# A hybrid decoder layer pair on one core: recurrent gates, norm sums and spreads placed between the last eight projection units, compression weights in eight pieces

## The chip, the core and the metric

One core of one Trainium2 chip runs the whole program in one launch. The metric is device time in microseconds (us) of that core. The engines are TensorE (PE; its weight loads are shown apart as PEld), VectorE (DVE), ScalarE (ACT), GpSimd (POOL) and SyncE (SP), which here only issues DMAs. The engines run their own instruction streams in order and meet at semaphores.

## What is computed

Two layers, each a mixer followed by a convolutional feed-forward part, over 320 tokens at once (256 of a prompt, and 8 sequences of 8 new tokens). Only the first mixer, a gated delta rule with 16 value heads and 8 key heads, and the compression weights of the second mixer are touched. In outline (q, k, v are slices of one projection; the recurrence is done in chunks):

```
h = rms_norm(x, gdn_norm)
qkv, z, b, a = split(h @ gdn_w_in)            # 4096 + 2048 + 16 + 16 columns
qkv = silu(causal_dwconv(qkv, conv_buf, conv_w))
q, k = l2norm(q) * DK ** -0.5, l2norm(k)      # over the 128 channels of a head
beta = sigmoid(b);  g = -exp(a_log) * softplus(a + dt_bias)
o = gated delta rule(q, k, v, g, beta, state) # per head; new states are outputs
y = (rms_norm(o) * out_norm * silu(z)) @ gdn_w_out
...
block = silu(blocks_of(past k or v, + cmp_pe) @ cmp_w1) @ cmp_w2     # second mixer
```

`cmp_pe` enters as a bias: `cmp_pe @ cmp_w1`, four columns of 128, is computed once.

## The kernel before, in words

The projection `gdn_in` is 24 units of 256 output columns (line 735 on). A unit is two lanes of 128 columns; each lane is 8 tiles of k times three products (lines 621 to 623: the float32 operands are split into a rounded high part and a low part), 48 matmuls of 320 columns a unit. For unit u, SP loads 1 MB of weights into one of four ring slots (L551), ACT rounds them (`high_part`, L582), DVE subtracts (`low_part`, L597). Units 0 to 15 give q, k and v (DVE runs three convolution taps a lane, L696), units 16 to 23 give z (ACT takes the silu, L784). The low part of unit u+2 is made while unit u is multiplied.

Then, in order:

- the `a` and `b` columns, 48 narrow products on PE (48 matmuls of 320 columns), semaphore `ab_done`; a barrier (`stage_closed`);
- the gates stage (`pe_gates`, `act_gates`, `dve_gates`, lines 832 to 942): ACT squares q and k in four groups, PE sums them over channels into one bank with one row a head (16 matmuls, L920), ACT root, DVE reciprocal, PE spreads each of 16 rows over 128 partitions (L926), DVE multiplies q and k by it (L878). Beside it the decay rows: exponents, logarithm, a scan, and PE turns them (L938). Between spreads 11 and 12 PE computes the bias of the compression from both halves of its weights (L1105), which SP loads from `ab_done` on (two 2 MB transfers, L1043);
- a second barrier; the core stage (`pe_core`, line 1217 on): eight pairs of heads, each a long chain between PE, DVE and ACT (`pe_core_pair`). In its gaps PE does the compression of one unit of past keys or values: eight groups of rows, each turned by PE (`turn_rows`, L1129), copied and rounded by ACT (L1190, L1193), its low part made by POOL (L1609), and multiplied by the compression weights in four pieces of three matmuls (`fill(lo, hi)` counts these pieces, 32 a pair, L1147). POOL first splits the weights (`split_w1`, L1603 and L1605), after the bias products have read them.

What a pair waits for by name: `rows` (decay rows spread over partitions, L1255, first read by DVE at L1476), `cp1` to `cx4` (eight steps on 32x32 blocks, L1278), `p, x, y` (L1290 to L1306), then the state products up to `snew` (L1373). Pair 0 is written out of the loop on PE and ACT and in the loop on DVE.

## Time and profile before

| what | us |
|---|---|
| runs | 1668.26, 1683.39, 1677.75 (median 1677.75) |
| profiled execution | 1667.57, of which the traced span 1665.9 |
| end of the last unit's products; end of the a and b products | 202.7; 209.7 |
| gates stage on PE, 209.7 to 246.8 | 37.1 |
| first `rows` read by DVE in pair 0, in pair 1 | 260.33, 311.78 |
| PE, DVE, ACT, POOL busy, whole span | 92%, 57%, 48%, 18% |

A row of a timeline gives the start, the duration, engine, source line, what is written from what, the count of instructions merged, and in brackets the idle time before and what ended it. A float32 matmul shows as two records. "Busy" of PE is modelled. The granted clock is the share of full speed (1.00 is 2.4 GHz, 0.50 is 1.2 GHz).

### The profile page before, as it was taken

To read this page: it belongs to the slowest core of one execution; us is meant where nothing else is said; L and a number is where in the kernel's file an instruction comes from. 1 tells how busy PE (TensorE), PEld (TensorE's weight loads), DVE (VectorE), ACT (ScalarE), POOL (GpSimd) and SP (SyncE) were. 2 spreads that over 40 slices of the span, in tenths; PEclk is the share of its full clock that TensorE was granted. 3 is DMA by queue.
4 is the path that set the end of the run, shared out by engine and by line. 5 is a ranking of instruction groups with operands and counts; after the bars stand their busy time and mean duration, and the time that the engine had idled before them with its cause. 6 is when DMAs were issued, how large, how long until landed. Compare 5 with 4: busy or idle time off the path is not lost. (4 is left out here: it accounts for less than half of the span.)

```text
span 1665.9 us, 37361 instructions
## 1 busy us (share of the span) xinstructions
PE 1525.8 (92%) x13678; PEld 1338.7 (80%) x13678; DVE 944.3 (57%) x1754; ACT 800.3 (48%) x1578; POOL 296.7 (18%) x492
## 2 busy tenths in 40 slices
PE   6999979999989999899999999987778869999896
PEld 6999947777767777589999999965556659999895
DVE  5776245555555555464777743535675557777631
ACT  5766235655565556543444532225555444444431
POOL 1332014433354333200000001032121100000000
PEclk9999978999999999979999999988997779999998
DMA  7445262344643443435555758555454324555640
GB/s 171 144 151 162 96 155 52 69 98 68 127 93 86 72 87 81 117 83 140 150 151 149 180 131 208 166 169 162 145 167 136 117 84 128 152 146 139 162 114 32
DMA packets 285314, 209.88 MB, mean 126 GB/s; under 512 B 29231, under 2 KB 277071, under 8 KB 284768
## 3 DMA queue, kind: packets, MB, share of 16 engines
q1 hardware_dynamic: 275926, 176.32, 40.6%
q0 software_dynamic: 9248, 31.80, 6.8%
q8 instruction: 63, 1.03, 0.3%
q10 hardware_dynamic: 42, 0.44, 0.1%
q14 instruction: 35, 0.29, 0.1%
HBM read 185.67 MB, written 22.85 MB: 125 GB/s over the span
## 5 line engine op out<-in xcount | busy, mean ns | idle before, releaser
L621 PE MATMUL psum<-h_rounded,weights_low 128*128 128x320 f32 x1248 | 392.0, 314 | 0.9 <-DVE weights_low L597 0.9
L623 PE MATMUL psum<-h_rounded,weights_high 128*128 128x320 f32 x1248 | 386.9, 310 | 0.0
L622 PE MATMUL psum<-weighted_x_low,weights_high 128*128 128x320 f32 x864 | 266.8, 309 | 0.0
L621 PEld LDWEIGHTS psum<-h_rounded,weights_low 128*128 128x128 f32 x1248 | 234.7, 188 | 4.1 <-DVE weights_low L597 1.2
L597 DVE TENSOR_TENSOR weights_low<-sbuf_resident,weights_high 128x2048 fp32r<-128x2048 f32 x90 | 205.7, 2287 | 52.2 <-ACT weights_high L582 52.1
L623 PEld LDWEIGHTS psum<-h_rounded,weights_high 128*128 128x128 f32 x1248 | 234.5, 188 | 0.0
L582 ACT CAST weights_high<-sbuf_resident 128x2048 fp32r<-128x2048 f32 x90 | 169.9, 1892 | 93.5 <-PE psum L623 64.1
L1190 ACT COPY sbuf_resident<-psum 64x256 f32<-64x256 f32 x256 | 108.5, 424 | 158.8 <-PE psum L1129 156.6
L622 PEld LDWEIGHTS psum<-weighted_x_low,weights_high 128*128 128x128 f32 x864 | 165.5, 192 | 0.2
L696 DVE SCALAR_TENSOR_TENSOR sbuf_stages<-sbuf_stages,sbuf_resident 128x344 f32<-128x344 f32 (+1 forms) x184 | 105.5, 574 | 55.7 <-ACT sbuf_stages L678 51.9
L678 ACT ACTIVATE sbuf_stages<-sbuf_stages,sbuf_resident 128x336 f32<-128x336 f32 (+1 forms) x76 | 44.1, 581 | 164.9 <-DVE sbuf_stages L1852 163.8
L1609 POOL TENSOR_TENSOR turned_low<-sbuf_resident,turned_high 128x512 fp32r<-128x512 f32 x64 | 76.7, 1199 | 249.6 <-ACT turned_high L1193 249.6
L622 PE MATMUL psum<-weights_low,weights_high 128*128 128x320 f32 x384 | 118.9, 310 | 0.0
L686 POOL COPY sbuf_stages<-sbuf_stages 128x2 f32<-128x2 f32 (+1 forms) x76 | 30.9, 407 | 488.5 <-DVE sbuf_stages L1852 411.7
L621 PE MATMUL psum<-hidden_high,weights_low 128*128 128x320 f32 x352 | 110.6, 314 | 6.6 <-ACT sbuf_resident L1809 5.7
L1147 PE MATMUL psum<-turned_high,w_low 128*128 128x504 f32 x256 | 109.2, 427 | 6.9 <-ACT turned_high L1193 6.4
L622 PE MATMUL psum<-hidden_low,weights_high_wide 128*128 128x320 f32 x352 | 109.7, 312 | 0.0
L623 PE MATMUL psum<-hidden_high,weights_high_wide 128*128 128x320 f32 x352 | 109.4, 311 | 0.0
L1147 PE MATMUL psum<-turned_high,w_high 128*128 128x504 f32 x256 | 103.5, 404 | 0.0
L1723 DVE TENSOR_TENSOR sbuf_resident<-sbuf_resident,psum 128x320 f32<-128x320 f32 x24 | 11.7, 487 | 119.6 <-PE psum L623 119.6
L1147 PE MATMUL psum<-turned_low,w_high 128*128 128x504 f32 x256 | 77.4, 404 | 0.0
L622 PEld LDWEIGHTS psum<-weights_low,weights_high 128*128 128x128 f32 x384 | 73.6, 192 | 0.0
(446 smaller groups left out, 3115.2 us busy)
## 6 DMA issues: line engine op xcount, KB each, us to landing
sbuf_resident<-in_ffn_w_up_dram SPq DMA_DIRECT2D x88, 512.0 KB, 5.0
sbuf_resident<-in_gdn_w_in_dram SPq DMA_DIRECT2D x48, 512.0 KB, 4.7
sbuf_resident<-in_ffn_w_down_dram SPq DMA_DIRECT2D x32, 704.0 KB, 5.8
sbuf_resident<-in_cache_nsa_kv_dram SPq DMA_DIRECT2D x256, 64.0 KB
sbuf_stages<-in_state_gdn_s_dram POOLq DMA_DIRECT2D x16, 512.0 KB, 8.7
out_gdn_s_sample_dram<-sbuf_stages SPq DMA_DIRECT2D x16, 512.0 KB, 3.8
sbuf_resident<-in_gdn_w_out_dram SPq DMA_DIRECT2D x16, 512.0 KB, 5.2
sbuf_stages<-in_cache_nsa_kv_dram POOLq DMA_DIRECT2D x64, 128.0 KB, 3.3
```

The lines of the kernel that those rows point to most:

```text
L582: act.copy(dst[:, 0:kn * P], slot(w)[:, 0:kn * P]).then_inc(hi_done, 1)
L597: eng.tensor_tensor(ring_lo[w % RING][:, 0:kn * P], sl, hi[:, 0:kn * P], ALU.subtract).then_inc(lo_done, 1)
L621: pe.matmul(out, w_lo, x_hi_tile, start=first, stop=False)
L622: pe.matmul(out, w_hi, x_lo_tile, start=False, stop=False)
L623: return pe.matmul(out, w_hi, x_hi_tile, start=False, stop=last)
L678: return act.activation(y[:, 0:n_out], xp[:, 0:n_out], ACT.Copy, scale=tap)
L686: pool.tensor_copy(tail[:, 0:hist], xp[:, TP:TP + hist])
L696: dve.scalar_tensor_tensor(out=y[:, 0:n_out], in0=xp[:, n:n + n_out], scalar=taps(n), in1=y[:, 0:n_out], op0=ALU.mult, op1=ALU.add).then_i ...
L1147: last = pe.matmul(psum[:, H_BANK[t], 0:4 * NC2], weights[:, 8 * half + m, t * P:(t + 1) * P], rows, start=(m == 0 and half == 0 and part ...
L1190: last = act.copy(dst, src)
L1609: return pool.tensor_tensor(turned_low[m % TURNED], turned[m % TURNED], turned_high[m % TURNED], ALU.subtract)
L1723: dve.tensor_tensor(xT[:, j, :], xT[:, j, :], bank(name, j, 1)[:, 0:T], ALU.add).then_inc(lane_free[1], 1)
```

## The change

Five edits.

1. The a and b products come right behind unit 16, and the gates stage is cut up and laid between units 17 to 23 (`pe_square_sums`, `pe_spread`, `pe_turn_gates` on PE; `act_squares`, `act_gate_exponents`, `act_root_and_log`, `act_decays` on ACT; DVE's chain with the low parts of units 18 to 23 in it). The barrier between the two stages goes.
2. The sums of squares are written to four groups of 32 partitions, the spreads read them from there: four matmuls of each go to four column or row groups of the array.
3. The bias: both halves of the weights are loaded in eight 512 KB pieces beside the units' weights, and DVE multiplies and adds their rows while units 7 to 10 and 12 to 15 run (`add_bias_rows`, 32 operations of 128x256); PE is left with four one-column matmuls.
4. The compression weights (keys) are then loaded once, in eight pieces, after unit 23, two ahead of the first raw rows and six behind. POOL splits a piece when it is in.
5. Pair 0 starts with its own chain: its turns and fills stand behind the eight steps of `cp` and `cx`. POOL loads the states of pair 0 at the start of the stage.

```diff
@@ pe_gdn_in, after the loop over the first 16 units
-            for u in range(4 * NQ + 1, 24):
-                unit(u // 4, u % 4)
...
             last.then_inc(ab_done, 1)
+            pe_square_sums(pe, 0)
+            pe_square_sums(pe, 1)
+            unit(4, 1)
+            pe_bias_columns(pe)
+            pe_square_sums(pe, 2)
+            pe_square_sums(pe, 3)
+            unit(4, 2)
+            unit(4, 3)
+            pe_spread(pe, 0)
+            unit(5, 0)
+            pe_spread(pe, 1)
+            unit(5, 1)
+            pe_spread(pe, 2)
+            multiply_unit(pe, "gdn_in", 5, 2, pair_tile, h_high, g_low_rounded, KD, lanes=(0,))
+            pe_spread(pe, 3)
+            multiply_unit(pe, "gdn_in", 5, 2, pair_tile, h_high, g_low_rounded, KD, lanes=(1,))
+            pe_turn_gates(pe)
+            unit(5, 3)
@@ act_gdn_in, the units of z
+                if j == NCT:
+                    act.wait_ge(bias_added.sem, bias_added.count("v0c15"))
...
+                    act_squares(act, 0)
+                    act_squares(act, 1)
+                    act_gate_exponents(act)
+                    act_squares(act, 2)
+                    act_squares(act, 3)
+                if j == NCT + 3:
+                    act.wait_ge(bias_pe, 1)
+                    act.copy(pe_bias, psum[:, 5, 508:512]).then_inc(bias_act, 1)
+                    act_root_and_log(act)
+                if j == NCT + 5:
+                    act_decays(act)
@@ dve_gdn_in
                 if l == 0:
                     low_part(dve, "gdn_in", u + 2, KD * 2)
-            for u in range(NCT // 2 + 2, 24):
-                low_part(dve, "gdn_in", u, KD * 2)
+                elif 7 <= u < 11:
+                    add_bias_rows(dve, 1, u - 7)
+                elif 12 <= u:
+                    add_bias_rows(dve, 0, u - 12)
+            dve_gates(dve)
@@ new on PE
+        def pe_square_sums(pe, a):
...
+            pe.wait_ge(S4["act"].sem, S4["act"].count(f"sq{a}"))
+            for c in range(4):
+                last = pe.matmul(psum[32 * c:32 * c + 32, 4, 0:T], pick_wide[:, 3 - a:35 - a], sq[a % 2][:, c, :], start=(a == 0), stop=(a == 3))
...
+        def pe_spread(pe, a):
...
+            for c in range(4):
+                r = slice(32 * c, 32 * c + 32)
+                last = pe.matmul(psum[:, 4 + c, 0:T], ident[r, 32 * c + a:32 * c + a + 1].to_broadcast([32, P]), inv_qk[r, :], start=True, stop=True)
@@ sp_compress
+            sp.wait_ge(unit_done, UNITS["gdn_in"][1])
+            for m in range(2):
+                load_w1(0, m)
+            load_raw(pages, 0, 0)
+            for m in range(2, 8):
+                load_w1(0, m)
+            load_raw(pages, 0, 1)
@@ pe_core
-            pe.wait_ge(pads, 11)
-            pe_bias_columns(pe)
-            pe.wait_ge(bias_act, 2)
-            turn_rows(pe, 0, 0, first=True)
+            pe.wait_ge(pads, 1)
             pe_core_pair(pe, 0, 0, "first")
@@ pe_core_pair, behind cx4
-            fill(20, 22)
+            if first:
+                turn_rows(pe, i, 0, first=True)
+                turn_rows(pe, i, 1)
+                fill(0, 4)
+                turn_rows(pe, i, 2, first=True)
+                fill(4, 6)
+            else:
+                fill(20, 22)
@@ the tensor block, and alike on the other engines
-            pe.drain().then_inc(stage_closed, 1)
-            pe.wait_ge(stage_closed, 4 * 2)
-            pe_gates(pe)
-            pe.drain().then_inc(stage_closed, 1)
+            pe.drain().then_inc(stage_closed, 2)
```

In pair 0 the other fills follow as 6 to 8, 8 to 11, 11 to 13, 13 to 17, 17 to 21, 21 to 25, 25 to 28, 28 to 32 behind the steps `p5`, `y5`, `p6`, `vtok`, `v0`, `s1`, `ks1`, `v1`.

DVE, the convolution part in units 6 to 8. Taps are L696, low parts L597. Before:

```order
L696 SCALAR_TENSOR_TENSOR sbuf_stages<-sbuf_stages,sbuf_resident 128x344 x6
L597 TENSOR_TENSOR weights_low_49<-sbuf_resident,weights_high_53 128x2048
L696 SCALAR_TENSOR_TENSOR sbuf_stages<-sbuf_stages,sbuf_resident 128x344 x6
L597 TENSOR_TENSOR weights_low_50<-sbuf_resident,weights_high_54 128x2048
L696 SCALAR_TENSOR_TENSOR sbuf_stages<-sbuf_stages,sbuf_resident 128x344 x6
```

Now (L892 and L889 are `add_bias_rows`):

```order
L597 TENSOR_TENSOR weights_low_50<-sbuf_resident,weights_high_54 128x2048
L696 SCALAR_TENSOR_TENSOR sbuf_stages<-sbuf_stages,sbuf_resident 128x344 x3
L892 TENSOR_SCALAR sbuf_stages<-sbuf_stages 128x256
L889 SCALAR_TENSOR_TENSOR sbuf_stages<-sbuf_stages 128x256 x3
L696 SCALAR_TENSOR_TENSOR sbuf_stages<-sbuf_stages,sbuf_resident 128x344 x3
L597 TENSOR_TENSOR weights_low_51<-sbuf_resident,weights_high_55 128x2048
L696 SCALAR_TENSOR_TENSOR sbuf_stages<-sbuf_stages,sbuf_resident 128x344 x3
L889 SCALAR_TENSOR_TENSOR sbuf_stages<-sbuf_stages 128x256 x4
```

Four operations of 128x256 now stand behind the second lane's taps of each of eight units.

DVE, the gates. Before (all low parts are done ahead of these rows):

```order
L869 TENSOR_SCALAR sbuf_stages<-sbuf_stages 16x320
L871 TENSOR_SCALAR sbuf_stages<-sbuf_stages 16x320
L874 RECIPROCAL sbuf_stages<-sbuf_stages 16x320
L881 RECIPROCAL sbuf_stages<-sbuf_stages 16x320
L878 SCALAR_TENSOR_TENSOR sbuf_stages<-psum,sbuf_stages 128x320 x8
```

Now:

```order
L947 TENSOR_SCALAR sbuf_stages<-sbuf_stages 16x320
L949 TENSOR_SCALAR sbuf_stages<-sbuf_stages 16x320
L952 RECIPROCAL sbuf_stages<-sbuf_stages 16x320
L597 TENSOR_TENSOR weights_low_52<-sbuf_resident,weights_high_56 128x2048
L955 RECIPROCAL sbuf_stages<-sbuf_stages 128x320
L957 TENSOR_TENSOR sbuf_stages<-sbuf_stages 16x320
L959 TENSOR_SCALAR sbuf_stages<-sbuf_stages 16x320
L961 SCALAR_TENSOR_TENSOR sbuf_stages<-sbuf_resident,sbuf_stages 16x320
L964 TENSOR_TENSOR sbuf_stages<-sbuf_stages 16x256
L967 TENSOR_TENSOR sbuf_stages<-sbuf_stages 16x64
L597 TENSOR_TENSOR weights_low_49<-sbuf_resident,weights_high_53 128x2048
L975 SCALAR_TENSOR_TENSOR sbuf_stages<-psum,sbuf_stages 128x320 x4
```

The low parts of units 19 and 20 now stand behind gate steps that wait for ACT and PE.

PE, the start of pair 0. Before (L1129 turns rows, L1147 fills, L1245 and L1251 are the products of keys and queries, L1255 the `rows`):

```order
L1129 MATMUL psum<-sbuf_resident 128x128 x4
L1245 MATMUL psum<-sbuf_stages 128x128 x4
L1129 MATMUL psum<-sbuf_resident 128x128 x4
L1147 MATMUL psum<-turned_high_72,w_low 128x504
L1147 MATMUL psum<-turned_high_72,w_high 128x504
L1147 MATMUL psum<-turned_high_72,w_low 128x504
L1251 MATMUL psum<-sbuf_stages 128x64 x2
L1255 MATMUL psum<-head_rows_65,ones_rounded 128x320
```

Now:

```order
L1307 MATMUL psum<-sbuf_stages 128x128 x4
L1314 MATMUL psum<-sbuf_stages 128x64 x2
L1318 MATMUL psum<-head_rows_65,ones_rounded 128x320
L1318 MATMUL psum<-head_rows_66,ones_rounded 128x320
L1318 MATMUL psum<-head_rows_65,ones_rounded 128x320
L1318 MATMUL psum<-head_rows_66,ones_rounded 128x320
L1328 MATMUL psum<-sbuf_resident,sbuf_stages 128x128 x3
L1340 MATMUL psum<-sbuf_resident 32x8
L1344 MATMUL psum<-sbuf_resident 32x32 x24
```

No turn and no fill is left in front of the first steps.

## Rows read from the trace of the kernel before

**Rows 1.** Engines from 209.7 to 246.8: busy us per engine, clock, DMA share, GB/s.
```profile
209.70:246.83 37.13, 31.24 (x143) 15.98 (x142) 17.57 (x33) 13.27 (x16) 3.33 (x4) 0.75 0.64 166
```

**Rows 2.** PE timeline, 202 to 254 us.
```profile
202.74 0.30 PE L621 MATMUL psum<-h_rounded,w_ab_low 128*16 128x320 f32 x1
...
212.94 8.80 PE L920 MATMUL psum<-sbuf_stages 128*16 128x320 f32 x32 [3.10 <-ACT sbuf_stages L843]
224.52 12.68 PE L926 MATMUL psum<-sbuf_stages,sbuf_resident 16*128 16x320 f32 x24 [2.79 <-DVE sbuf_stages L881]
237.13 6.10 PE L1105 MATMUL psum<-sbuf_resident,sbuf_stages 128*32 128x256 f32 x64
...
245.42 1.09 PE L938 MATMUL psum<-sbuf_resident,sbuf_stages 16*128 16x16 f32 x12
...
252.06 1.87 PE L1113 MATMUL psum<-sbuf_resident 128*128 128x2 f32 x8 [5.23 <-DVE sbuf_stages L1471]
```

**Rows 3.** DVE timeline in units 13 to 15.
```profile
131.65 2.29 DVE L597 TENSOR_TENSOR weights_low<-sbuf_resident,weights_high 128x2048 fp32r<-128x2048 f32 x1
...
137.06 1.80 DVE L696 SCALAR_TENSOR_TENSOR sbuf_stages<-sbuf_stages,sbuf_resident 128x344 f32<-128x344 f32 x3 [1.40 <-ACT sbuf_stages L678]
...
146.05 2.29 DVE L597 TENSOR_TENSOR weights_low<-sbuf_resident,weights_high 128x2048 fp32r<-128x2048 f32 x1
```

**Rows 4.** DVE timeline, gates and pair 0.
```profile
222.33 2.14 DVE L881 RECIPROCAL sbuf_stages<-sbuf_stages 16x320 f32<-16x320 f32 x1 [8.00 <-ACT sbuf_stages L851]
...
226.57 0.49 DVE L878 SCALAR_TENSOR_TENSOR sbuf_stages<-psum,sbuf_stages 128x320 f32<-128x320 f32 x1 [0.58 <-PE psum L926]
...
247.85 2.42 DVE L1458 TENSOR_SCALAR head_rows<-sbuf_stages,sbuf_resident 48x640 fp32r<-48x640 f32 x2 [0.25 <-DVEq L2988]
...
251.08 0.92 DVE L1471 COPY sbuf_stages<-sbuf_resident 64x64 f32<-64x64 f32 x2
260.33 0.89 DVE L1476 TENSOR_TENSOR sbuf_stages<-psum,sbuf_resident 128x320 f32<-128x320 f32 x2 [8.33 <-PE psum L1255]
...
268.21 0.38 DVE L1505 STREAM_TRANSPOSE sbuf_resident<-sbuf_resident 128x192 f32<-128x192 f32 x1
...
311.78 0.89 DVE L1476 TENSOR_TENSOR sbuf_stages<-psum,sbuf_resident 128x320 f32<-128x320 f32 x2 [1.47 <-PE psum L1255]
```

**Rows 5.** PE timeline in pair 0.
```profile
269.62 0.62 PE L1278 MATMUL psum<-sbuf_resident 32*32 32x32 f32 x48
...
282.10 0.94 PE L1147 MATMUL psum<-turned_low,w_high 128*128 128x504 f32 x3
...
283.35 0.39 PE L1147 MATMUL psum<-turned_high,w_low 128*128 128x504 f32 x1
283.57 0.39 PE L1147 MATMUL psum<-turned_high,w_high 128*128 128x504 f32 x1
...
284.93 1.18 PE L1290 MATMUL psum<-sbuf_stages 128*128 128x128 f32 x8 [0.52 <-DVE sbuf_stages L1534]
```

**Rows 6.** Engines in stretches of 4 us: PE, PEld, DVE, ACT, POOL, clock, DMA, GB/s.
```profile
218.00:222.00 4.00, 3.73 (x14) 1.15 (x12) 0.00 (x0) 3.06 (x5) 0.00 (x0) 1.00 1.10 348
...
226.00:230.00 4.00, 4.00 (x8) 2.46 (x8) 1.70 (x4) 0.00 (x0) 0.00 (x0) 0.50 0.08 23
...
254.00:258.00 4.00, 3.81 (x17) 3.39 (x17) 0.00 (x0) 3.25 (x8) 3.84 (x5) 0.50 0.00 0
258.00:262.00 4.00, 4.00 (x21) 3.24 (x20) 1.55 (x5) 3.09 (x7) 3.50 (x4) 0.85 0.00 0
```

**Rows 7.** SP timeline: the 32 transfers of the first raw rows.
```profile
228.22 15.36 SPq L1054 DMA_DIRECT2D sbuf_resident<-in_cache_nsa_kv_dram  x32
```

**Rows 8.** ACT timeline: a group of turned rows copied and rounded.
```profile
268.21 1.73 ACT L1190 COPY sbuf_resident<-psum 64x256 f32<-64x256 f32 x4 [1.49 <-PE psum L1129]
269.98 0.62 ACT L1193 CAST turned_high<-sbuf_resident 128x512 fp32r<-128x512 f32 x1
```

**Rows 9.** POOL timeline: the second half of the last piece of weights split.
```profile
257.76 1.28 POOL L1605 TENSOR_TENSOR w_low<-sbuf_resident,w_high 128x512 fp32r<-128x512 f32 x1
```

More of the change, by code:

```diff
@@ L824, in build @@
         ea = space.take(1, parts=VH)
-        sq = [space.take(4, T) for _ in range(2)]
-        inv_qk = space.take(T, parts=VH)
-        C_G, C_B, C_E, C_N = range(4)
-        S4 = dict(pe=steps("gates_pe", [f"sum{g}" for g in range(4)] + [f"wide{j}" for j in range(VH)] + ["turned"]),
-                  dve=steps("gates_dve", ["pad", "zero", "dt", "relu", "den", "beta", "inv"] + [f"out{j}" for j in range(8)] + ["soft", "g", "scan", "gap0", "gap"]
-                            + [f"out{j}" for j in range(8, 12)] + ["nb", "high", "low"] + [f"out{j}" for j in range(12, VH)] + ["tok", "toks"]),
-                  act=steps("gates_act", ["nbexp", "sq0", "sq1", "sq2", "sq3", "abs", "expn", "root", "log", "ea", "egap", "eg"]))
@@ L833, in act_gates @@
-        def act_gates(act):
+        inv_qk = space.take(T)
+        bias_sum = space.take(2, CHID, off=core + CONV_CH)
+        assert space.at <= core + CONV_CH and core + CONV_CH + 2 * CHID <= hi_at
+        bias_w = space.take(4, 4, CHID, off=core - 16 * CHID)
+        sq = [space.take(4, T, off=core - 8 * T + 4 * T * x) for x in range(2)]
+        bias_w_in = [sem(f"bias_weights_in{q}") for q in range(4)]
+        bias_added = steps("bias_rows_added", [f"v{v}c{c}" for v in (1, 0) for c in range(16)])
@@ new lines, in build @@
+        bias_pe, bias_act = sem("pe_bias_product"), sem("pe_bias_copied")
+        gate_tables = sem("gate_tables")
+        C_G, C_B, C_E, C_N = range(4)
+        S4 = dict(pe=steps("gates_pe", [f"sum{g}" for g in range(4)] + [f"wide{a}" for a in range(4)] + ["turned"]),
+                  dve=steps("gates_dve", ["pad", "zero", "dt", "relu", "den", "beta", "inv", "soft", "g", "scan", "gap0", "gap"] + [f"out{j}" for j in range(8)]
+                            + ["nb", "high", "low"] + [f"out{j}" for j in range(8, VH)] + ["tok", "toks"]),
+                  act=steps("gates_act", ["sq0", "sq1", "nbexp", "abs", "expn", "ea", "sq2", "sq3", "root", "log", "egap", "eg"]))
@@ new lines, in pe_bias_columns, with act_squares @@
+        def pe_bias_columns(pe):
+            for v in range(2):
+                for t in range(2):
+                    last = pe.matmul(psum[:, 5, 508 + 2 * v + t:509 + 2 * v + t], bias_sum[:, v, t * P:(t + 1) * P], ones[:, 0:1], start=True, stop=True)
+            last.then_inc(bias_pe, 1)
+        def act_squares(act, a):
+            if a >= 2:
+                act.wait_ge(S4["pe"].sem, S4["pe"].count(f"sum{a - 2}"))
+            act.activation(sq[a % 2], qkv[:, 4 * a:4 * a + 4, :], ACT.Square).then_inc(S4["act"].sem, S4["act"].step(f"sq{a}"))
@@ L844, in act_gates @@
-            for g in range(4):
-                squares(g)
             act.wait_ge(dve_steps.sem, dve_steps.count("dt"))
@@ L1307, in pe_core_pair @@
                     last.then_inc(pe_steps.sem, pe_steps.step(f"y{k}{h}"))
-                if k == SMALL:
+                if k == SMALL and not first:
                     turn_rows(pe, i, 6)
+                elif k == SMALL:
+                    fill(8, 11)
             for h in range(2):
```

300 lines of the change are left out of this document (178 added, 122 removed).

## The prediction

> **What bounds the kernel now.** I read the page's slices first, then the stretch between the last projection unit and pair 1 of the core stage, since every edit lies there or in its cover. Within the units PE never waits: 48 matmuls of 320 columns take 6.96 us (202.74 to 209.70), and that is both the a and b products and one unit [rows 1, 2]. From 209.7 to 246.83 nothing dense runs. PE waits 3.10 us for the first squares and 2.79 us for the reciprocal; the sums take 8.80 us; the spreads go at 1.07 us each because a spread, its semaphore and DVE's 0.49 us multiplication alternate (DVE idles 0.58 us before each) [rows 2, 4]. The clock has fallen to one half by 226, so the stretch has a mean of 0.75 [rows 1, 6]. These 37.1 us are a chain of small steps on three engines, not work. A second such stretch follows: from the barrier at 247.85 to the first read of the `rows` at 260.33 (12.5 us), of which PE spends 5.23 us waiting for DVE's padding writes, then 1.87 us on bias columns, then turns and fills at half clock ahead of the `rows` [rows 2, 4, 6]. From there a pair takes 51.45 us (260.33 to 311.78) and PE is nearly full; its idle before `p5` is 0.52 us [rows 4, 5].
>
> So a microsecond is worth a microsecond at PE up to about 260, and after that only if PE's own work or its waits in pair 0 shrink.
>
> **The gates, moved under the units.** Seven units stay, and the 6.96 us of a and b products only change place. Added to PE's stream between them:
> - 16 sums. In one row group they took 8.80 us for 16, so 0.55 each. The bias products (L1105) are the nearest row for four column groups: 32 matmuls of 256 columns in 6.10 us, mostly at half clock, 0.19 us each, where one after the other 256 columns would cost 0.55 x 256/320 = 0.44 us even at full clock. Four therefore do run at once, and four sums cost about 0.6 us: 2.4 in all. Bounds 2.2 and 8.8.
> - 16 spreads in four row groups, same size: 2.6 us. The row for 32-deep products with all groups is the small blocks (48 records in 0.62 us [rows 5]). Bounds 2.2 and 8.8.
> - bias columns: 1.87 us at half clock, so 0.9; turns 1.09 and one more product, 1.4.
>
> With 1 us for gaps that is 8.3 us against 37.1: **28.8 us saved**.
>
> What hides the rest. ACT has the bias wait, the copy and the two stores of the convolution rows and two squares to do before the first sums; laid one behind the other from the end of unit 16 they take about as long as the a and b products. A bare tie, and the 1 us for gaps is mostly for it. DVE now has low parts behind gate steps: that of unit 19 stands behind the exponents and a reciprocal (2.14 us), that of unit 20 behind root, logarithm and scan, those of 21 to 23 behind the multiplications of a spread. Laying 2.29 us for a low part, 2.14 for a reciprocal and 4 x 0.45 for a spread's multiplications behind the PE step that releases them [rows 3, 4], each low part is done 2 to 9 us before PE reaches its unit; the closest is unit 22: spread 1 is followed by a unit of 6.96 us, while DVE needs 1.8 + 1.8 (decay rows) + 2.3 = 5.9. If one were late, every us of it would be a us of PE.
>
> **The bias on DVE.** An operation of 128x344 that waits for the one before has a pitch of 0.60 (1.80 for three); 88 elements fewer at 0.96 GHz leave 0.51, so four cost 2.0 us. DVE idles 1.40 us per unit there [rows 3], so each of eight units puts it 0.6 us behind, with 1.4 won back at unit 11. The tightest is the low part of unit 17, behind seven of them: 7 x 0.63 - 1.4 = 3.0 us late. It ends at 148.34 now, and unit 17 starts at 202.74 - 7 x 6.96 = 154.0, which is 5.7 us of cover. Nothing reaches PE; the cover is gone at (5.7 + 1.4) / 7 + 1.4 = 2.4 us a unit, 0.60 an operation, so it is not wide. Bounds: 0.27 (256 elements, no wait) and 0.60 (the bigger operation's pitch): nothing on the path at either. The 4 MB more of loads lie beside 8 of the units' 1 MB each; I cost them at nothing since four slots of the ring stand between a load and its unit.
>
> **The start of pair 0.** The bias columns, two turns and one fill leave it. After the barrier DVE needs 2.42 us for the two rows and 1.6 us for padding, and PE has its products ready by then: 4.1 us instead of 12.5, **8.4 saved**.
>
> **Pair 0 itself is lengthened.** All 32 fills remain (each three matmuls of 0.22 to 0.23 us, 0.68 [rows 5]), but none stands before `cx4`. Up to there the chain is DVE's, and PE's fills now and then stood in front of a step: 0.9 us at the first (`x0` ends at 268.59, the blocks start at 269.62, 0.16 of it their first small product), 3.8 us over all eight. So `cx4` ends 18.0 instead of 21.8 us behind the first read (282.10 - 260.33) [rows 4, 5]. Then two turns follow with ACT between them: turn 0.5, copy 1.73, turn, rounding 0.62, and each hand-over [rows 8], then six fills (4.1) before `p5`: 7.75 us behind `cx4` against 2.8 before. From `p5` to the next pair 26.85 us become 37: 16 more fills (10.9), three more turns (1.3), less 2 us of idle that they fill. Sum 18.0 + 7.75 + 37 = 62.7 us against 51.45: **11.3 lost** at full clock.
>
> Transfers: 16 raw loads take 7.7 us of SP [rows 7]; the six later weight pieces land some 15 us after unit 23, POOL splits each in about 1.9 us (1.28 for the second half [rows 9]), done 24 us after unit 23. The first fill comes at 26. Close, but covered, the more so if pair 0 is slowed.
>
> **The clock.** In the trace the clock stays full while the sums run, and is at one half at 226, 16 us after the last dense product; it is back between 258 and 262, some 5 us after PE became dense at 254 [rows 6]. Pair 0 has now a first part with PE almost idle: after unit 23 the `rows`, then nothing for 8 us (260.33 to `x0` at 268.6), then small blocks. I expect half clock from about `cp1` to 5 us into the fills. Eight steps of 0.71 or 0.54 us would double: up to 5.0; dense fills for 5 us at half speed: 2.5. I take **6.5 lost**, bounds 0 and 7.5. The Trainium skill (TensorE: Matmul & The Clock Gate, section on the HAM clock gate) says that an idle array falls back to 1.2 GHz and only activity releases it. By that rule the products at the start of pair 0 could be cold too, about 1.5 us more than my sum; the trace agrees as far as it shows the fall after sparse work.
>
> **Sum.** 28.8 + 8.4 - 11.3 - 6.5 = 19.4 us. The profiled execution of 1667.57 becomes 1648.2. The three runs and the profiled one have a mean of 1674, and the median of the runs is 10 us above the profiled one; I put the forecast at the middle of these levels: **1654 us**. A measurement of this kernel can tell about 1% (17 us) from no change; the gain sits just above that.
>
> **Rivals.**
> - *The clock holds through pair 0* (for it: it held from 210 to 222 through the sums; against: PE is emptier now). Gain 26: 1648.
> - *A new wait takes over between the units*: a low part of units 19 to 23 late, or ACT's squares behind the stored rows. For it: DVE and ACT run in order, and ACT's root and exponents stand before roundings of weights that PE needs soon; against: 2 to 9 us of cover each. At 1 to 2 us in five gaps it costs 8: gain 11, 1663.
> - *The packed sums and spreads run one after the other*: 6.4 + 6.2 us more: gain 7, 1667. Against: L1105.
> - *Slower*: the bias operations contend with the low parts and convolution on DVE. Past 0.60 us each, the 28 ahead of unit 17's low part reach PE one for one. The whole gain is gone at 0.60 + 19.4/28 = 1.3 us; 1% slower at 1.9 us. The rows have 0.60 for a bigger operation, so little speaks for it.
> - *The stage start doesn't move* because the first raw rows or weights come late: fills would stall 5 us; it acts as the second rival.
>
> **How the numbers follow.** Forecast 0.45; clock holds 0.15; new wait 0.25; packing fails 0.06; slower 0.04; start late 0.05. Faster by over 1%: three quarters of the forecast, all of the second, a tenth or so of the rest: 0.56, rounded up to 0.58 since the levels of runs scatter both ways; slower 0.05; same 0.37. The range leaves out little more than the outer tenth on each side: low 1640 (clock holds, at the level of the profiled execution, less 1 to 2 us of small terms), high 1670 (a new wait or failed packing at the level of the median).
>
> **What would show it.** Right: the last unit's products end near 218, PE's idle between units under 1 us; the four sums of a group take about 0.6 us; the first `rows` are read by DVE near 223; clock 0.5 between about 232 and 250; pair 1's first read near 292. Wrong: PE waiting for a low part behind a spread; DVE's operations of 128x256 above 0.6 us; pair 0 above 72 us; PE waiting for POOL's split at the first fills.

## The result and the profile after

| | before | after |
|---|---|---|
| median of 20 runs each, same chip | 1677.62 us | 1656.11 us |
| ratio after to before, 95% interval | | 0.9838 (0.9809 to 0.9866) |
| span of the profiled execution, mean clock | 1665.9 us, 0.951 | 1638.8 us, 0.957 |
| last unit's products end | 202.7, a and b 209.7 | 218.5 |
| first read of `rows`, pair 0 / pair 1 | 260.33 / 311.78 | 222.70 / 295.79 |

The ratio leaves out eight of the 20 executions after, those more than 1.5% above the fastest; the medians of all twenty differ by 21.5 us, a ratio of 0.987. So the change makes the kernel 1.3 to 1.6% faster, clear of noise, and the median is within 2 us of the forecast. Up to pair 1 the profiled execution gained 16.0 us; the rest of its 27 comes later and is taken up at the end.

The page after, first lines:

```profile
span 1638.8 us, 37162 instructions
PE 1491.6 (91%) x13614; PEld 1318.8 (80%) x13614; DVE 953.9 (58%) x1788; ACT 804.0 (49%) x1581; POOL 303.6 (19%) x492
```

PE timeline after, the gates between the units (L1002 sums, L897 bias columns, L1013 spreads), the last unit's last product (L623), then pair 0 (L1344 the 32x32 products of `cp` and `cx`, L1192 a turn, L1364 `p5`):

```profile
161.03 1.28 PE L1002 MATMUL psum<-sbuf_stages,sbuf_resident 128*32 128x320 f32 x16
169.34 0.95 PE L897 MATMUL psum<-sbuf_resident,sbuf_stages 128*128 128x1 f32 x8
170.21 1.28 PE L1002 MATMUL psum<-sbuf_stages,sbuf_resident 128*32 128x320 f32 x16
...
193.53 0.82 PE L1013 MATMUL psum<-sbuf_stages,sbuf_resident 32*128 32x320 f32 x8
...
218.23 0.30 PE L623 MATMUL psum<-h_rounded,weights_high 128*128 128x320 f32 x1
...
229.90 0.24 PE L1340 MATMUL psum<-sbuf_resident 128*32 128x8 f32 x2 [5.29 <-DVE sbuf_resident L1617]
230.07 0.86 PE L1344 MATMUL psum<-sbuf_resident 32*32 32x32 f32 x48
...
233.59 0.54 PE L1344 MATMUL psum<-sbuf_resident 32*32 32x32 f32 x23
239.00 0.58 PE L1344 MATMUL psum<-sbuf_resident 32*32 32x32 f32 x25 [4.87 <-issue]
...
246.54 0.65 PE L1344 MATMUL psum<-sbuf_resident 32*32 32x32 f32 x32
...
250.18 1.12 PE L1192 MATMUL psum<-sbuf_resident 128*128 128x128 f32 x4 [1.94 <-ACT sbuf_resident L1253]
...
257.92 1.05 PE L1364 MATMUL psum<-sbuf_stages 128*128 128x128 f32 x8
```

Eight sums take 1.28 us, where 16 took 8.80 [rows 2]. In pair 0 a step of 48 records (the small products of one `cp` or `cx`, two records each) takes 0.86 instead of 0.62 [rows 5], and at 234 PE stops inside one such group for 4.87 us. No semaphore stands there: 23 of 48 records are done, the other 25 come 4.87 us later, and the releaser is "issue". This is called the stop below.

DVE timeline after (L889 a bias operation, L597 the low part of unit 17, L1588 the reads of `rows`):

```profile
99.97 2.04 DVE L889 SCALAR_TENSOR_TENSOR sbuf_stages<-sbuf_stages 128x256 f32<-128x256 f32 x4
...
147.26 2.28 DVE L597 TENSOR_TENSOR weights_low<-sbuf_resident,weights_high 128x2048 fp32r<-128x2048 f32 x1
...
222.70 0.89 DVE L1588 TENSOR_TENSOR sbuf_stages<-psum,sbuf_resident 128x320 f32<-128x320 f32 x2 [1.30 <-PE psum L1318]
...
295.79 0.89 DVE L1588 TENSOR_TENSOR sbuf_stages<-psum,sbuf_resident 128x320 f32<-128x320 f32 x2 [1.47 <-PE psum L1318]
```

ACT timeline after, pair 0: the copies of v, then the first turned rows.

```profile
245.93 0.82 ACT L1526 COPY sbuf_stages<-sbuf_stages 128x320 f32<-128x320 f32 x2 [20.06 <-POOLq L1697]
...
248.43 1.70 ACT L1253 COPY sbuf_resident<-psum 64x256 f32<-64x256 f32 x4
```

ACT stood for 20.06 us: its copies of v wait for POOL's opening `sem_inc` (L1697), which stands behind all eight splits on POOL. The forecast did not have this wait.

Stretches of 4 us after (PE, PEld, DVE, ACT, POOL, clock, DMA share, GB/s), which answer to [rows 6]:

```profile
218.00:222.00 4.00, 2.15 (x18) 1.85 (x18) 2.01 (x13) 2.54 (x4) 0.47 (x1) 0.99 0.49 152
222.00:226.00 4.00, 1.54 (x7) 0.77 (x7) 3.30 (x10) 2.07 (x5) 3.24 (x4) 0.50 0.56 101
...
230.00:234.00 4.00, 2.63 (x125) 2.28 (x124) 2.91 (x11) 0.00 (x0) 0.00 (x0) 0.50 1.15 133
...
254.00:258.00 4.00, 4.00 (x17) 3.19 (x16) 0.00 (x0) 1.23 (x3) 2.32 (x3) 0.74 0.02 4
258.00:262.00 4.00, 4.00 (x32) 3.71 (x31) 1.56 (x4) 2.25 (x6) 1.29 (x1) 1.00 0.02 3
```

The clock is at one half from 222 to 254, ten microseconds sooner than forecast. The sums of the old gates had kept it full for 12 us [rows 6]; here PE is busy for 2.15 us of the 4 from 218 on and for 1.54 of the next 4.

### The profile page after: what moved, and what is told of

Read it like the earlier page. It is cut to its first block and busy times, and to the rows that moved or that the text cites. A ratio compares the mean times of both kernels' runs of the same rounds, so it can differ in the third digit from the quotient of the medians.

```text
span 1638.8 us, 37162 instructions
## 1 busy us (share of the span) xinstructions
PE 1491.6 (91%) x13614; PEld 1318.8 (80%) x13614; DVE 953.9 (58%) x1788; ACT 804.0 (49%) x1581; POOL 303.6 (19%) x492
## 5 line engine op out<-in xcount | busy, mean ns | idle before, releaser
L623 PE MATMUL psum<-h_rounded,weights_high 128*128 128x320 f32 x1248 | 386.7, 310 | 0.0
L623 PEld LDWEIGHTS psum<-h_rounded,weights_high 128*128 128x128 f32 x1248 | 234.6, 188 | 0.0
L597 DVE TENSOR_TENSOR weights_low<-sbuf_resident,weights_high 128x2048 fp32r<-128x2048 f32 x90 | 205.6, 2286 | 30.6 <-ACT weights_high L582 30.4
L696 DVE SCALAR_TENSOR_TENSOR sbuf_stages<-sbuf_stages,sbuf_resident 128x344 f32<-128x344 f32 (+1 forms) x184 | 105.5, 573 | 44.6 <-ACT sbuf_stages L678 40.8
L686 POOL COPY sbuf_stages<-sbuf_stages 128x2 f32<-128x2 f32 (+1 forms) x76 | 34.4, 453 | 481.9 <-DVE sbuf_stages L1972 412.0
L623 PE MATMUL psum<-hidden_high,weights_high_wide 128*128 128x320 f32 x352 | 109.5, 311 | 0.0
```

The costliest lines, as they stand in the source:

```text
L597: eng.tensor_tensor(ring_lo[w % RING][:, 0:kn * P], sl, hi[:, 0:kn * P], ALU.subtract).then_inc(lo_done, 1)
L623: return pe.matmul(out, w_hi, x_hi_tile, start=False, stop=last)
L686: pool.tensor_copy(tail[:, 0:hist], xp[:, TP:TP + hist])
L696: dve.scalar_tensor_tensor(out=y[:, 0:n_out], in0=xp[:, n:n + n_out], scalar=taps(n), in1=y[:, 0:n_out], op0=ALU.mult, op1=ALU.add).then_i ...
```

## The experiments

Each is read by three places in its profile: first read of `rows`, PE's stop without a releaser, first read in pair 1 (all in us from the start; pair 0 is the third less the first). Each profile is one execution, and whole times scatter by more than most of these differences.

| kernel | first read | stop | pair 1 | pair 0 |
|---|---|---|---|---|
| after | 222.70 | 4.87 | 295.79 | 73.1 |
| e1 POOL says ready first | 222.72 | 2.66 | 292.97 | 70.3 |
| e2 data behind `cx4` | 222.56 | none | 316.30 | 93.7 |
| e3 PE kept busy | 222.19 | 0.52 | 287.86 | 65.7 |
| e4 fills in the gaps | 222.56 | 5.95 | 293.87 | 71.3 |
| e5 both | 222.42 | none, 5.41 for rows | 288.98 | 66.6 |
| e6 both, weights late | 221.62 | none, 1.84 for rows | 286.25 | 64.6 |
| e7 old order of pair 0 | 245.13 | none, 20.39 for rows | 301.03 | 55.9 |
| e8 gates behind units | 244.23 | none | 311.60 | 67.4 |
| e9 rows early, old order | 239.01 | none, 11.00 for a split | 299.07 | 60.1 |
| e10 rows early, with e5 | 222.02 | 5.31 | 291.85 | 69.8 |
| e12 rows early, with e1 | 222.51 | 2.12 | 291.67 | 69.2 |
| e13 half early, old order | 225.57 | none | 279.20 | 53.6 |

**ACT's unpriced wait (e1).**

```diff
+            pool.sem_inc(S5["pool"].sem, S5["pool"].first - 1)
             for m in range(8):
                 split_w1(pool, 0, m)
...
         def pool_core(pool):
-            pool.sem_inc(S5["pool"].sem, S5["pool"].first - 1)
```

> POOL's opening sem_inc, for which ACT's copies of v wait, goes ahead of the eight splits; nothing else changes. ACT should copy v near 226 instead of 246 (its wait of 20.06 us goes). Theory: that wait cost almost nothing, since PE reached the first turn only at 247.12 and ACT's copy of it began at 248.43, right behind its work on kdec; pair 0 stays 72 to 74 us and a PE stop of 4 to 5 us without a releaser is there again among the 32x32 products. Rival: ACT's wait was what pair 0 hung on; then pair 0 gets 4 us or more shorter (69 or less).

ACT copied v at 225.79, 20 us sooner. Pair 0 got 2.8 us shorter, and 2.2 of that is the stop, which was 2.66 us in this execution:

```profile
233.58 0.54 PE L1344 MATMUL psum<-sbuf_resident 32*32 32x32 f32 x23
236.78 0.58 PE L1344 MATMUL psum<-sbuf_resident 32*32 32x32 f32 x25 [2.66 <-issue]
```

So the wait was worth at most 0.6 us, as expected; pair 0 fell below the expected 72 to 74 because the stop is not a constant. Its place is: again behind the 23rd record.

**What the stop is (e2).**

```diff
             for m in range(2):
                 load_w1(0, m)
+            sp.wait_ge(S5["pe"].sem, S5["pe"].count("cx4", 0))
             load_raw(pages, 0, 0)
```

> SP issues two pieces of weights as before, then waits for PE's cx4 of pair 0 before the raw rows and the other six pieces, so hardly a transfer runs under the 32x32 products. A diagnosis, not an improvement: pair 0 grows by 15 to 25 us. Theory A, the PE stop of 4.87 us without a releaser is instructions that arrive late behind the data: the stop goes (below 1 us) and first read to end of cx4 is 19 to 20 us instead of 24.4. Theory B, it is a fixed price of new code or something of PE's own: a stop of 4 to 5 us stays there, 24 us in all. The granted clock should be half either way.

PE timeline of e2, and one stretch of 4 us:

```profile
233.33 0.86 PE L1345 MATMUL psum<-sbuf_resident 32*32 32x32 f32 x48
...
241.18 0.65 PE L1345 MATMUL psum<-sbuf_resident 32*32 32x32 f32 x32
...
256.12 1.12 PE L1193 MATMUL psum<-sbuf_resident 128*128 128x128 f32 x4 [14.28 <-DMA sbuf_resident<-in_cache_nsa_kv_dram]
```

```profile
230.00:234.00 4.00, 2.63 (x148) 2.31 (x142) 2.65 (x10) 0.00 (x0) 0.00 (x0) 0.50 0.01 4
```

The same PE code over a DMA share of 0.01 runs its 48 records through in 0.86 us, and `cx4` ends 19.3 us behind the first read instead of 24.5. Theory B falls: without transfers there is no stop, and e8 below, with a share of 0.03 or less beside the same steps, has none either. Transfers alone do not make a stop, though. The kernel before ran all eight steps of pair 0 without one, over a share that rose from 0.10 to 0.90:

```profile
274.00:278.00 4.00, 4.00 (x141) 2.89 (x128) 1.45 (x5) 2.06 (x5) 1.80 (x2) 1.00 0.59 97
278.00:282.00 4.00, 4.00 (x114) 2.85 (x112) 1.02 (x4) 1.69 (x4) 1.44 (x2) 1.00 0.90 145
```

So did e7 and e9, over 0.4 to 0.6 for most of the steps. The second condition seems to be a place in the code: the stop stands behind record 23 of `cp2` in the kernel after, e1, e4 and e12, and elsewhere once products are added ahead of it (e3 and e10). Within one order its length goes with the transfers: 5.95 us in e4 (share 1.07 from 234 to 238), 4.87 in the kernel after (0.88), 2.66 in e1 (0.58), 2.12 in e12 (0.15). That it is the arrival of the next instructions, held up behind data, fits all of this, but it is inferred: no view shows the load itself as late, and no run moved the place of the code alone. The Trainium skill (Runtime: NRT & Kernel Launch, section on instruction fetch mechanics) says that an engine's instructions are refilled block by block through a DMA queue of its own, at a cost that is "mostly hidden". If the stop is such a refill, it is not hidden here: 4.87 us among small products, beside a DMA share of 1.15 and then 0.88.

**The clock (e3).** On e1:

```diff
+        def warm(pe, n):
+            for _ in range(n):
+                pe.matmul(psum[:, H_BANK[0], 0:T], ident, const("strict3"), start=True, stop=True)
...
+            warm(pe, 2)
             pe.wait_ge(pads, 1)
...
+                    if first and n < 19:
+                        warm(pe, 1)
```

> e1 plus products that nothing reads (ident with strict3, 320 columns, into a free bank) wherever PE waits in pair 0: 2 at the stage's start, 2 before bts1, 9 before x0, 1 before each cp and cx step, 3 between turns 0 and 1. Theory, the half clock costs pair 0 some 5 us (9 steps of 32x32 products at 0.86 and 0.65 instead of 0.62 and 0.45: 1.9 us; transposes, turns and fills at 0.42 instead of 0.23 between 247 and 254.5: 3 to 4): the granted clock stays 1.00 from 220 to 258 and pair 0 is 67 to 70 us; in the whole about 0.3% faster than the changed kernel. Rival, the clock is no cost there since PE waits for DVE and ACT anyway: pair 0 stays 72 to 74. Rival, the added products are in the way: pair 0 above 74.

```profile
235.74 0.34 PE L1352 MATMUL psum<-sbuf_resident 32*32 32x32 f32 x17
236.59 0.32 PE L1352 MATMUL psum<-sbuf_resident 32*32 32x32 f32 x15 [0.52 <-issue]
...
240.46 0.45 PE L1352 MATMUL psum<-sbuf_resident 32*32 32x32 f32 x32
...
247.20 1.18 PE L1210 MATMUL psum<-turned_low,w_high 128*128 128x504 f32 x4 [1.10 <-POOL turned_low L1735]
...
250.03 1.05 PE L1375 MATMUL psum<-sbuf_stages 128*128 128x128 f32 x8
```

(The diff shows three of the places; the expectation lists all.) The clock stays at 1.00 from 218 on. Without their stops pair 0 is 67.6 us in e1 and 65.1 here: the half clock cost 2.4 us, or 3.5 when the 1.10 us for POOL's low part is counted, which the earlier fills ran into. Pair 0 as measured, 65.7 us, is below the expected 67 to 70, since the stop was only 0.52 us. The whole is 0.9856 of before (0.9742 to 0.9971), which can't be told from the changed kernel.

**The order (e4, e5).** On e1: turn 0 behind `cp2`, turn 1 behind `cp3`, fills behind the last three steps; POOL splits a piece ahead of each low part. e5 has the added products too.

```diff
+                    elif n == 14:
+                        turn_rows(pe, i, 0, first=True)
+                    elif n == 16:
+                        turn_rows(pe, i, 1)
+                    elif n > 16:
+                        fill(n - 17, n - 16)
             if first:
-                turn_rows(pe, i, 0, first=True)
-                turn_rows(pe, i, 1)
-                fill(0, 4)
+                fill(3, 4)
```

> e1 plus pair 0's turn 0 behind cp2, turn 1 behind cp3, fills 0, 1 and 2 behind cx3, cp4 and cx4, with POOL splitting two pieces, then one before each low part. Theory, the work that stands in a row between cx4 and p5 (10.8 us) is what lengthened pair 0, and gaps of PE hide it: cx4 to p5 falls to 3 to 5 us, the steps before it grow by 1 to 3, pair 0 is 66 to 70 us, the whole 0.2 to 0.4% faster than the changed kernel. Rival, the raw rows land later than cp2 (issued 219.66 to 226.97, landing 9 to 10 us later): PE waits for them at turn 0 and pair 0 stays within 2 us of 73.

`cx4` to `p5` fell from 10.7 to 4.5 us (251.55 to 256.07), and pair 0 without its stop from 67.6 to 65.4. But the stop was 5.95 us this time, and behind it PE still waited for the raw rows:

```profile
239.82 0.58 PE L1344 MATMUL psum<-sbuf_resident 32*32 32x32 f32 x25 [5.95 <-issue]
...
241.16 1.12 PE L1192 MATMUL psum<-sbuf_resident 128*128 128x128 f32 x4 [0.77 <-DMA sbuf_resident<-in_cache_nsa_kv_dram]
```

So the rows were in at about 241, not some 9 us behind their issue. Pair 0 as measured, 71.3 us, missed the expected 66 to 70. Ratio 0.9895 (0.9783 to 1.0006), which shows no gain over the changed kernel.

> The last two edits together: turns 0 and 1 and fills 0 to 2 between the steps of 32x32 products, and products that nothing reads in the waits of PE that are left (2 at the start, 2 before bts1, 9 before x0, 1 behind cp1, cx1 and before cx2). Theory: the two savings add up, since one is the clock and the other the order: without the PE stop pair 0 was 67.6 us with neither, 65.2 with the clock, 65.4 with the order; both give 63, plus a stop of 0.5 to 6 us for which nothing is done here: 63.5 to 69. Rival: at full clock the gaps are too short for a fill, which then delays DVE's chain; pair 0 stays at 65 to 66 without the stop.

PE waited 5.41 us for the rows (until 238.84), and what the two edits save does not add up while the rows set the time. A stop behind a wait like this one would not be seen, so the "none" of e5 is no evidence on the stop. Ratio 0.9859 (0.9740 to 0.9979).

**Late weights (e6).** On e5:

```diff
             load_raw(pages, 0, 0)
+            sp.wait_ge(S5["pe"].sem, S5["pe"].count("cx2", 0))
             for m in range(2, 8):
```

> As the kernel with both, and SP holds weight pieces 2 to 7 and the second raw rows until PE's cx2, so that nothing but the first raw rows is under way when PE reaches the place (23rd product of cp2) where it stopped four times for 4.87, 2.66, 5.95 and (at another count) 0.52 us. Theory: the stop is instructions arriving behind that data, so it is below 0.5 us and pair 0 is 62 to 64 us; pieces land by 246 and are not waited for. Rival: POOL's splits or the second raw rows now come late and PE waits for them at fills 8 to 16: pair 0 above 66.

No stop is seen, PE does not wait for the later pieces, and pair 0 is 64.6 us, just above the expected 62 to 64. The rows still hold turn 0 for 1.84 us, until 234.76, although only the states of pair 0 (1 MB) were loaded beside them. As in e5, that wait could hide a short stop. Ratio 0.9889 (0.9813 to 0.9965).

**The order undone (e7).** On e1, `first = False` in the pair's functions, turn 0 ahead of the pair, and POOL's splits as in e4.

> Only the order of pair 0 goes back to that of before (turn 0 ahead of the pair, turn 1 and fill 0 ahead of the `rows`, the others as in pairs 1 to 7), on the kernel in which POOL splits a piece ahead of each low part. Theory: the first raw rows are in at 236 to 241 (PE waited for them until 241.2 in the kernel with fills in the gaps), so the first read of `rows` moves from 223 to 242 to 247, pair 0 is 51 to 54 us again, and pair 1 starts at 295 to 300: the new order is worth 2 to 5 us against 293. Rival, the forecast's view of the loads (rows in about 231): first read at 236, pair 1 at 288, and the new order costs 5 us.

```profile
239.41 1.09 PE L1192 MATMUL psum<-sbuf_resident 128*128 128x128 f32 x4 [20.39 <-DMA sbuf_resident<-in_cache_nsa_kv_dram]
```

The first read comes where expected; pair 0 is 55.9 us in the old order, 2 more than thought, so the new order is worth 8.1 us (292.97 against 301.03) and not 2 to 5, and 10.7 if e1's stop is taken off. It is worth that because the rows are late; in e13 below, where the first rows come in time, the old order is ahead.

**The gates undone (e8).** Edit 1 alone, on the kernel after (the squares and the bias sum get other memory):

```diff
+            for u in range(4 * NQ + 1, 24):
+                unit(u // 4, u % 4)
             pe.wait_ge(ab_split, 2)
...
+            for a in range(4):
+                pe_square_sums(pe, a)
             pe_bias_columns(pe)
...
+            for a in range(4):
+                pe_spread(pe, a)
             pe_turn_gates(pe)
```

> The gates stand behind unit 23 again, and the a and b products too, but in the packed form, with the bias on DVE, the loads behind and the new pair 0. Theory: the units end at 202.7, a and b at 209.7, and the chain of squares, root, reciprocal (2.15), four rounds of spread and four multiplications (about 2.7 each) and turns takes 24 to 28 us: first read of `rows` at 238 to 242, 15 to 19 us later than in the changed kernel, pair 0 shorter by 1 to 5 since loads are in earlier. So of the 28.8 us that the forecast gave to the gates, 9 to 13 are from packing and the bias on DVE, the rest from cover. Rival: nearly all is packing, and the first read comes by 232.

```profile
213.23 2.45 PE L992 MATMUL psum<-sbuf_stages,sbuf_resident 128*32 128x320 f32 x16 [2.78 <-ACT sbuf_stages L892]
...
221.76 1.45 PE L1003 MATMUL psum<-sbuf_stages,sbuf_resident 32*128 32x320 f32 x8 [4.28 <-DVE sbuf_stages L945]
```

The first read comes at 244.23, 2 us later than expected; from 214 on the chain ran at half clock. Of the 37.6 us between 260.33 and 222.70, 16.1 come from packing, the bias on DVE and the shorter start, 21.5 from the cover of the units. Pair 0 takes 67.4 us, since no stop falls into it, and pair 1 starts at 311.60, where before has it (311.78). The new order of pair 0 thus spent what packing had won. The one time of the whole, 1658.81 us, says nothing about these edits.

**Where the rows spend their time (e9, e10, e12).** The ring slots of units 21 and 22 are free one and two units before the end. With the raw rows placed there and the split weights laid around them, the rows can be loaded under the units:

```diff
-        raw = [space.take(8, KV_DIM, off=at + x * 8 * KV_DIM) for x in range(2)]
+        raw = [space.take(8, KV_DIM, off=ring_at + (1 + x) * SLOT) for x in range(2)]
...
+            for x in range(2):
+                sp.wait_ge(unit_done, UNITS["gdn_in"][1] - 2 + x)
+                load_raw(pages, 0, x)
             sp.wait_ge(unit_done, UNITS["gdn_in"][1])
-            for m in range(2):
+            for m in range(8):
                 load_w1(0, m)
-            load_raw(pages, 0, 0)
-            for m in range(2, 8):
-                load_w1(0, m)
-            load_raw(pages, 0, 1)
```

> The memory of the compression stage is laid out anew (raw rows in the ring slots of units 21 and 22, the split weights around them), so that the first raw rows are loaded when unit 21 is done and the second when unit 22 is done; only the weight pieces wait for unit 23. Pair 0 in the old order, POOL's split of a piece ahead of each low part. Theory: what held the old order to a first read at 245.13 was 20.4 us of waiting for the raw rows; with them in by 219, turn 0 runs at once and the first fill waits for the first split (223 to 224): first read at 226 to 229, pair 0 51.5 to 55 us as before, pair 1 at 278 to 283, that is 13 to 18 us earlier than in the changed kernel; the whole 0.8 to 1.1% faster than the changed kernel, 2.4 to 2.8% than before. Rival: POOL (splits of 1.9 us each, eight, with low parts between) now sets pair 0: PE waits for splits or low parts, pair 0 60 or more, pair 1 at 287 or later. Rival: the loads disturb units 22 and 23: the last unit ends later than 219.

SP timeline and two stretches of e9:

```profile
201.23 16.42 SPq L1133 DMA_DIRECT2D sbuf_resident<-in_cache_nsa_kv_dram  x32
218.07 13.64 SPq L1154 DMA_DIRECT2D sbuf_resident<-in_nsa_cmp_w_dram  x8
```

```profile
208.00:212.00 4.00, 4.00 (x36) 3.76 (x35) 0.69 (x3) 0.44 (x1) 0.00 (x0) 1.00 0.57 77
224.00:228.00 4.00, 0.77 (x4) 0.53 (x4) 0.00 (x0) 2.75 (x6) 0.00 (x0) 0.93 1.16 113
```

This was the miss that explained the rest. Alone, the rows move at 77 GB/s with a DMA share of 0.57: 2 MB need 27 us, not the 16.4 that their issue takes. The pieces issued at 218 queue behind them; the first split came at 233.76, and PE stood 11.00 us for it. The Trainium skill (DMA: Bandwidth & Descriptors, on how many engines a DMA uses) has a DMA from SP spread over a number of engines, 16 at most, that divides its outer dimension; a load of raw rows writes 8 partitions, so 8 of 16 engines by that rule, and the share of 0.57 lies near that half. No run loaded the same rows over more partitions, so this reason is argued, not shown. Ratio 0.9914 (0.9883 to 0.9945), clearly behind the forecast of 0.972 to 0.976.

> The same early rows under the order with fills in the gaps and products that nothing reads. Theory: the wait of 5.4 us for the raw rows at turn 0 is gone, the clock is full throughout, no stop of PE: pair 0 59 to 62 us after a first read at 222, pair 1 at 282 to 285, later than with the old order since 20 fills still stand behind p5. Rival: the stop without a releaser comes back (it was hidden in the wait): 285 to 289.

> The early rows alone, on the kernel in which POOL tells ACT first, order of pair 0 as in the changed kernel. Only the 2 MB of weight pieces are under way after unit 23, in by about 228. Theory, the stop of PE (2.66 to 5.95 us so far, none without transfers) is instructions behind data: it is below 1 us, pair 0 66.5 to 68 us, pair 1 at 289 to 291. Rival, the pieces alone are enough to hold the instructions: stop of 2 us or more, pair 0 70 or more.

PE timeline of e10, then of e12:

```profile
236.58 0.31 PE L1355 MATMUL psum<-sbuf_resident 32*32 32x32 f32 x3 [5.31 <-issue]
```

```profile
235.93 0.58 PE L1347 MATMUL psum<-sbuf_resident 32*32 32x32 f32 x25 [2.12 <-issue]
```

Both met the stop, and both missed what was expected: 5.31 us behind record 45 of `cx1` in e10, where the DMA share was 1.13 from 230 to 234, and 2.12 behind record 23 of `cp2` in e12, where it was 0.79. Pair 1 of e10 starts at 291.85, later than even its rival had it (285 to 289), and e12's at 291.67, just behind the expected 289 to 291. That the pieces are in by 228, as e12's expectation has it, fell with the same rows. e10's ratio is 0.9887 (0.9837 to 0.9937).

**One half early (e13).** The layout of e9, the pair order of e7, and only the first rows ahead. Against e9 three more things change: five products that nothing reads, one split ahead of each low part, and states that are loaded later.

```diff
+            sp.wait_ge(unit_done, UNITS["gdn_in"][1] - 2)
+            load_raw(pages, 0, 0)
             sp.wait_ge(unit_done, UNITS["gdn_in"][1])
-            for m in range(2):
-                load_w1(0, m)
-            load_raw(pages, 0, 0)
-            for m in range(2, 8):
+            for m in range(8):
                 load_w1(0, m)
             load_raw(pages, 0, 1)
```

> The new memory layout, but only the first raw rows go ahead (behind unit 21), then, behind unit 23, the eight weight pieces, then the second raw rows; pair 0 in the old order, turn 0 as the first thing, POOL one split ahead of each low part, the states where the other pairs load them, 5 products that nothing reads in two of PE's waits. The first raw rows alone took 13 us (1 MB at 77 GB/s), so from 201.3 they are in at 215, and the pieces no longer queue behind rows, as they did when the first split came at 233.76. Theory: piece 0 is in at 221.5, split by 223.5; first read of `rows` at 225 to 228, pair 0 52 to 55 us with a stop of at most 3, pair 1 at 277 to 283, which is 13 to 18 us ahead of the changed kernel (295.79); the whole 0.97 to 0.98 of before, 0.8 to 1% faster than the changed kernel, if the clock in the later stages is like. Rival: raw rows 4 to 7 come too late behind the pieces (issued to 231, in at 240, first needed at about 240), or POOL's splits do: PE waits 3 to 8 us, pair 1 at 283 to 288. Rival: the first piece still lands after 226, first read at 230 or later, pair 1 at 285 or later.

SP, POOL and DVE timelines of e13:

```profile
201.42 7.50 SPq L1133 DMA_DIRECT2D sbuf_resident<-in_cache_nsa_kv_dram  x16
218.27 3.99 SPq L1154 DMA_DIRECT2D sbuf_resident<-in_nsa_cmp_w_dram  x8
...
221.13 0.62 POOL L1733 CAST w_high<-sbuf_resident 128x512 fp32r<-128x512 f32 x1 [71.34 <-DMA sbuf_resident<-in_nsa_cmp_w_dram]
...
225.57 0.89 DVE L1603 TENSOR_TENSOR sbuf_stages<-psum,sbuf_resident 128x320 f32<-128x320 f32 x2 [4.47 <-PE psum L1329]
...
279.20 0.89 DVE L1603 TENSOR_TENSOR sbuf_stages<-psum,sbuf_resident 128x320 f32<-128x320 f32 x2 [1.47 <-PE psum L1329]
```

```profile
222.00:226.00 4.00, 4.00 (x23) 3.09 (x21) 0.43 (x2) 3.76 (x7) 3.92 (x4) 1.00 0.97 317
234.00:238.00 4.00, 2.72 (x60) 1.73 (x58) 3.93 (x8) 3.72 (x11) 2.75 (x3) 1.00 0.09 26
...
246.00:250.00 4.00, 4.00 (x83) 3.02 (x81) 1.81 (x5) 2.31 (x5) 2.64 (x4) 1.00 1.02 231
```

The pieces go out in 3.99 us instead of 13.64 and arrive at 317 GB/s; the first is split from 221.13 on; the clock is 1.00 throughout. The first blocks run under a DMA share of 0.09, the last two steps, from 246.5 on, under 1.02, and none of them stops. Pair 1 starts at 279.20, 16.6 us ahead of the changed kernel and 32.6 ahead of before, as expected; at the start of the attention stage, at 1071.50 us, 12.7 and 29.3 of this are left. The median is 1639.00 us, the ratio to before **0.9737 (0.9693 to 0.9782)**, about 1% better than the changed kernel's 0.9838, with intervals that do not meet (1.2% better by the medians of all executions). It beats both. The placement of the loads explains the first read; how much of the rest is the clock that the five products kept at 1.00 was not taken apart.

## Why the prediction held, and where it did not

- **Gates between units: right.** Forecast 8.3 us added to PE up to the last unit's end, measured 8.8 (209.7 to 218.5). In packed form the 16 sums took 2.56 us (2.4 forecast), the spreads 3.3 (2.6). PE waits for nothing between 150 and 218. The low part of unit 17 ends at 149.54, 1.2 us later than before where 3.0 was forecast, and a bias operation takes 0.51 us, as worked out. The rivals of a new wait there, of failed packing, and of DVE as the bound fell.
- **Start of pair 0: right.** First read at 222.70 against 223.
- **Pair 0: right in sign, too small.** 73.1 us against 69.2. At full clock and without its stop, e3 has 18.2 us to the end of `cx4` (forecast 18.0), 8.0 to `p5` (7.75, POOL's 1.10 taken off), 37.8 to pair 1 (37). So the serial part was worked out well: 64.0 against 62.7. With 3.5 for the clock, 4.9 for the stop and 0.6 for ACT's wait that makes 73.0 of the measured 73.1.
- **The clock: mechanism right, size wrong.** It fell at 222, not 232, and cost 2.4 to 3.5 us where 6.5 was taken. The step that failed is the doubling of eight steps, up to 5.0 us in the sum. The four longer ones grew from 0.62 to 0.86 us and the four shorter ones from 0.45 to 0.65, 1.8 in all, and the waits for DVE between them did not double.
- **What was missing: the stop of 4.87 us.** [rows 5] could not show it: before, the same steps ran through whole beside transfers (share 0.59 and 0.90 from 274 to 282). One stop of 1.13 us stands in pair 1, outside the rows that the forecast read. The forecast asked only whether loads arrive in time, not what else they may hold up. The two errors, 3 to 4 us too much for the clock and 4.9 too little for the stop, largely cancel. That is luck. With the serial part 1.3 us too short and the 0.6 of ACT's wait they leave pair 0 3.9 us longer than forecast. With 0.4 us more than forecast won up to the first read, that is the 16.0 us gained at pair 1 against 19.4.
- **Transfers: a wrong step without a price.** The forecast had POOL done 24 us behind unit 23, just ahead of the first fill at 26. It was done at 247.2, 28.7 behind, and PE was late too. "Land some 15 us after" took every byte as equal; the raw rows are the slow ones. In e7, PE waits 20.39 us for them before the old order can start, and in e9 it waits 11.00 us for weights queued behind them.
- **The whole time: near by luck too.** The forecast set its gain of 19.4 us against a level of 1674. The level of before measured 1677.6, and the gain by medians is 21.5, of which places show 16.0.
- **The rest of the gain.** At the start of the attention stage the profiled execution is 16.6 us ahead, at its end 27.0. No edit touches that stage. Its length in before, after and e4 (PE, PEld, DVE, ACT, POOL, clock, DMA share, GB/s), first before:

```profile
1100.79:1371.84 271.05, 211.46 (x2474) 153.80 (x2474) 156.17 (x394) 137.00 (x388) 46.80 (x84) 0.86 0.46 147
```

```profile
1084.17:1344.82 260.65, 200.74 (x2473) 145.53 (x2474) 155.97 (x394) 136.45 (x388) 46.68 (x84) 0.91 0.48 153
```

```profile
1084.97:1369.76 284.79, 225.81 (x2474) 164.03 (x2474) 156.15 (x394) 137.20 (x388) 46.67 (x84) 0.81 0.44 140
```

The same instructions take 260.65 to 284.79 us as the clock goes from 0.91 to 0.81. So 10.4 us of the profiled 27 are that stage's length in two executions, which goes with its clock. Mean clocks are known for 36 further executions of before and for the 20 after. In both sets an execution is about 10 to 11 us longer for each 0.01 of clock less. At a mean clock of 0.945 a straight line through each set gives 1674 and 1654 us, an estimate from these runs: 20 us, or 1.2%, which the clock's luck does not explain. Of these, 16.0 to 16.6 are shown by place, and 4 were not traced to an edit. The 0.9838, some 27 us, is then on the high side.

## What to carry to other kernels

When a barrier goes, ask what the transfers that start there now run beside: their issue time, their rate, and the small operations that an engine runs just then. A slow transfer pattern (here 1 MB of rows at 77 GB/s) is worth starting early, even if the layout has to be turned around for it. It should not stand ahead of a fast one that is waited for first, as 2 MB of it did in e9. Judge a few microseconds by the position of a fixed event in the trace; whole times of this kernel move by more than that through the clock of a stage that no edit touches.
